# Three attentions: all turns of a pair in one place, the third and fourth group in the main banks, outputs turned back one pair later

## What is computed

```python
# window: 8 query heads, keys within 128 positions and 256 context keys, a sink column per head
s = where(|i - j| <= 128, q @ k.T * 64**-0.5, NEG);  p = softmax([s, s_ctx, sink])[..., :-1];  y = p @ v
# grid: 8 heads, keys in a neighbourhood of rows and columns, with a bias, and 256 context keys
s = q @ k.T * 64**-0.5 + bias;  p = softmax([s, s_ctx]);  y = p @ v
# dilated: 8 heads, a mixture of three dilations, written as one softmax over all earlier keys with log-multiplicities added
s = q @ k.T + log(multiplicity);  p = softmax(s);  y = p @ v
```

## Time and profile before

| | |
|---|---|
| Median of 3 runs | 2650.97 us (2650.01 to 2652.58) |
| Profiled execution | 2643.95 us, its span 2642.0 us |
| Granted TensorE clock, mean | 0.996 of 2.4 GHz |
| PE busy | 2573.2 us, 97% of the span |
| PEld busy | 1870.0 us, 71% |
| DVE, ACT, POOL busy | 58%, 30%, 8% |
| Chain that ended last | PE 92%, DVE 3%, issue 2%, ACT 2% |

### The profile page before, as it was taken

One profiled execution on the slowest core, in us unless ns is written; L12 is line 12 of the kernel. 1 busy time (PEld: TensorE's weight loads), 2 busy tenths in 40 slices (PEclk: granted clock), 3 DMA queues, 4 the chain that ended last, 5 costly groups with the idle time before them and its releaser, 6 DMA issues.

```text
span 2642.0 us, 37526 instructions
## 1 busy us (share of the span) xinstructions
PE 2573.2 (97%) x14026; PEld 1870.0 (71%) x14026; DVE 1539.8 (58%) x3920; ACT 804.4 (30%) x1740; POOL 223.7 (8%) x401
## 2 busy tenths in 40 slices
PE   6999999999999999999999999999999999999999
PEld 3577688777778685466688776868578766555867
DVE  2357677599866663434353476657868664515554
ACT  3236511176721123322210066113312264121210
POOL 1100000000011000000051031200000002002000
PEclk9999999999999999999999999999999999999999
DMA  7121000022013230211001110523240103316231
GB/s 275 36 79 48 21 33 32 32 73 73 18 52 108 66 106 28 100 41 41 9 25 38 50 34 30 92 80 107 85 144 32 68 18 98 119 53 250 95 113 56
DMA packets 73059, 188.78 MB, mean 71 GB/s; under 512 B 6988, under 2 KB 9744, under 8 KB 71952
## 3 DMA queue, kind: packets, MB, share of 16 engines
q0 software_dynamic: 26656, 94.84, 11.2%
q1 hardware_dynamic: 45472, 91.16, 9.9%
q10 hardware_dynamic: 752, 0.38, 0.1%
HBM read 143.69 MB, written 43.01 MB: 71 GB/s over the span
## 4 chain that ended last, share of the span: by engine, by line
PE 92%; DVE 3%; issue 2%; ACT 2%; DMA 0%; ACTq 0%; POOL 0%; DVEq 0%
PE psum L1378 36%; PE psum L1710 11%; PE psum L1650 8%; PE psum L1722 7%; PE psum L1740 5%; PE psum L1806 4%; PE psum L1737 4%; PE psum L1592 3%; PE psum L1492 3%; PE psum L1364 2%; PE psum L1345 1%; PE psum L1878 1%; PE psum L1896 1%; PE psum L1865 1%; PE psum L1625 1%
## 5 line engine op out<-in xcount | busy, mean ns | idle before, releaser
L3167 ACT ACTIVATE RP<-RP,small 128x1280 f32<-128x1280 f32 (+11 forms) x274 | 252.0, 920 | 165.4 <-DVE small L2725 161.5
L1710 PE MATMUL psum<-RQ 64*128 64x256 f32 (+5 forms) x1344 | 294.0, 498 | 2.0 <-DVE small L2725 1.2
L2725 DVE CUSTOM_DVE_ANT_0 RP<-psum,small 128x512 f32<-128x512 f32 (+1 forms) x382 | 201.8, 573 | 109.0 <-PE psum L1722 86.5
L1650 PE MATMUL psum<-RW,hT 128*128 128x512 f32 (+2 forms) x640 | 237.8, 527 | 1.0 <-ACT hT L2917 1.0
L1722 PE MATMUL psum<-ident,RP 128*128 128x128 f32 x1388 | 206.2, 283 | 9.1 <-DVE RP L2738 4.5
L1722 PEld LDWEIGHTS psum<-ident,RP 128*128 128x128 f32 x1388 | 151.3, 142 | 82.1 <-issue 68.5
L3179 ACT ACTIVATE RP<-psum 128x512 f32<-128x512 f32 (+1 forms) x288 | 150.1, 521 | 192.3 <-PE psum L1722 182.0
L1710 PEld LDWEIGHTS psum<-RQ 64*128 64x128 f32 (+1 forms) x1344 | 140.5, 189 | 88.2 <-issue 48.2
L1650 PEld LDWEIGHTS psum<-RW,hT 128*128 128x128 f32 x640 | 135.2, 215 | 87.5 <-issue 69.8
L1378 PE MATMUL psum<-RW,hT 128*128 128x256 f32 x864 | 195.9, 379 | 0.0
L1378 PEld LDWEIGHTS psum<-RW,hT 128*128 128x128 f32 x864 | 163.8, 190 | 25.0 <-issue 2.2
(11 more groups left out here) (485 smaller groups left out, 3937.1 us busy)
## 6 DMA issues: line engine op xcount, KB each, us to landing
RW<-in_w_in SPq DMA_DIRECT2D x7, 2048.0 KB, 8.0
RW<-in_od_w_ada SPq DMA_DIRECT2D x6, 2048.0 KB, 7.9
RW<-in_ev_w_in SPq DMA_DIRECT2D x5, 2048.0 KB, 7.7
RW<-in_od_w_in SPq DMA_DIRECT2D x5, 2048.0 KB, 7.9
RQ<-in_ev_w_ada SPq DMA_DIRECT2D x4, 2048.0 KB, 19.7
RX<-in_x POOLq DMA_DIRECT2D x12, 512.0 KB, 7.3
y_even<-YR POOLq DMA_DIRECT2D x20, 256.0 KB, 2.3
RP<-y_even POOLq DMA_DIRECT2D x20, 256.0 KB, 3.5
```

The source lines that it names most:

```text
L1650: last = pe.matmul(main.bank(f)[:, 0:nc_], lhs_of(st["lhs"], j["t"], kk), w, start=kk == 0, stop=kk == kn - 1)
L1710: last = pe.matmul(main.bank(f)[:, 0:pc["w"]], q, kk[:, keys], start=i == 0, stop=i == len(u["qk"]) - 1)
L2725: drained(main, dve.tensor_tensor_reduce(pair_slot(st, u, lane)[:, pc["at"]:pc["at"] + pc["w"]], main.bank(f)[:, 0:pc["w"]], add, -scale, ...
L3167: fn(pr, pr, ACT.Exp, bias=mins[:, at, lane, n - 1:n], scale=-1.0, accum_out=sums[:, at, lane:lane + 1]).then_inc(s_pexp, 1)
```

## The change

In the three attentions all chunks of a pair are turned in one place, behind the values of the pair before. The first two are fills of `turn` as before, the third and fourth are fills of `main`, numbered after the scores of the next pair. The first and third chunk are copied by ACT, the second and fourth by DVE. The turn-back of pair i - 2 (not i - 1) stands at the end of the round, and the last two pairs' turn-backs stand behind the loop. Each chunk now carries its ring (`ch["ring"]`), and all waits on chunks go through it. The latent attention keeps its loop, from which the branches of the other three are taken out; diff keeps its own.

The plan:

```diff
                 for c in range(n):
-                    side = "act" if c % 2 or (n == 3 and c == 2) or kind == "diff" else "dve"
-                    u["turns"].append({"f": turn.new(side), "c": chunk_count[0], "tiles": tiles[cuts[c]:cuts[c + 1]]})
+                    ch = {"ring": turn, "c": chunk_count[0], "tiles": tiles[cuts[c]:cuts[c + 1]]}
+                    if kind in HALVES and c >= 2:
+                        ch["ring"] = main
+                    elif kind in HALVES:
+                        ch["f"] = turn.new("dve" if c else "act")
+                    else:
+                        ch["f"] = turn.new("act" if c % 2 or (n == 3 and c == 2) or kind == "diff" else "dve")
+                    u["turns"].append(ch)
...
-                if at and kind in HALVES:
-                    pairs[at - 1]["back"] = main.new("dve")
+                if kind in HALVES:
+                    for c, ch in enumerate(u["turns"][2:]):
+                        ch["f"] = main.new("dve" if c else "act")
+                    if at >= 2:
+                        pairs[at - 2]["back"] = main.new("dve")
             if kind in HALVES:
-                pairs[-1]["back"] = main.new("dve")
+                for u in pairs[-2:]:
+                    u["back"] = main.new("dve")
```

PE:

```diff
+                    if k in HALVES:
+                        for i, u in enumerate(ps):
+                            for nxt in ps[i + 1:i + 2]:
+                                scores(nxt, nxt["pieces"])
+                            if i:
+                                pair_values(ps[i - 1], slice(None))
+                            for nxt in ps[i + 1:i + 2]:
+                                if nxt["aside"]:
+                                    modulation(*nxt["aside"])
+                            for ch in u["turns"]:
+                                turn_chunk(u, ch)
+                            if i >= 2:
+                                turn_back(ps[i - 2])
+                        turn_back(ps[-2])
+                        pair_values(ps[-1], slice(None))
+                        turn_back(ps[-1])
+                        continue
```

DVE and ACT:

```diff
+                    if k in HALVES:
+                        for i, u in enumerate(ps):
+                            for nxt in ps[i + 1:i + 2]:
+                                for c in range(len(nxt["pieces"])):
+                                    for lane in range(2):
+                                        minima(nxt, lane, c)
+                                if nxt["aside"]:
+                                    modulation(*nxt["aside"])
+                            divide(u)
+                            turned_chunks(u, u["turns"])
+                            if i >= 2:
+                                pair_y(ps[i - 2])
+                        for u in ps[-2:]:
+                            pair_y(u)
+                        continue
...
+                    if k in HALVES:
+                        for i, u in enumerate(ps):
+                            for nxt in ps[i + 1:i + 2]:
+                                exponential(nxt, 0)
+                            if i:
+                                pair_outputs(ps[i - 1])
+                            turned_chunks(u, u["turns"])
+                            for nxt in ps[i + 1:i + 2]:
+                                exponential(nxt, 1)
+                        pair_outputs(ps[-1])
+                        continue
```

More of the change, by code:

```diff
@@ L527, in plan_pairs @@
                 for c in range(n):
-                    side = "act" if c % 2 or (n == 3 and c == 2) or kind == "diff" else "dve"
-                    u["turns"].append({"f": turn.new(side), "c": chunk_count[0], "tiles": tiles[cuts[c]:cuts[c + 1]]})
+                    ch = {"ring": turn, "c": chunk_count[0], "tiles": tiles[cuts[c]:cuts[c + 1]]}
[6 more added lines that the diff above has]
+                    u["turns"].append(ch)
                     chunk_count[0] += 1
-                u["turned"] = [[ch["f"] for ch in u["turns"] if any(x[0] == lane for x in ch["tiles"])][-1:] for lane in range(2)]
+                u["turned"] = [[ch for ch in u["turns"] if any(x[0] == lane for x in ch["tiles"])][-1:] for lane in range(2)]
             def number_scores(u):
@@ L1192, in sink_columns @@
                         if u["at"] >= 3:
-                            turn.wait_full(gp, ps[u["at"] - 3]["turns"][-1]["f"])
+                            ch = ps[u["at"] - 3]["turns"][-1]
+                            ch["ring"].wait_full(gp, ch["f"])
                         else:
@@ L1719, in turn_chunk @@
                             pe.wait_ge(s_pexp, 2 * u["g"] + 1 + max(x[0] for x in ch["tiles"]))
-                        turn.wait_free(pe, ch["f"])
+                        ring = ch["ring"]
+                        ring.wait_free(pe, ch["f"])
                         for i, (lane, at, _) in enumerate(ch["tiles"]):
-                            last = pe.transpose(turn.bank(ch["f"])[:, i * P:(i + 1) * P],
+                            last = pe.transpose(ring.bank(ch["f"])[:, i * P:(i + 1) * P],
                                                 pair_slot(st, u, lane)[:, at:at + P], ident[:, :])
-                        turn.written(last)
+                        ring.written(last)
                     def pair_values(u, chunks):
@@ L1730, in pair_values @@
                         for ch in u["turns"][chunks]:
-                            turn.wait_drained(pe, ch["f"])
+                            ch["ring"].wait_drained(pe, ch["f"])
                             for i, (lane, at, kt) in enumerate(ch["tiles"]):
@@ L1786, in _ @@
                             turn_chunk(u, ch)
-                        if before and k in HALVES:
-                            turn_back(before)
                     for ch in ps[-1]["turns"][2:4]:
                         turn_chunk(ps[-1], ch)
[L1791 to L1796, removed]
+                    pair_values(ps[-1], slice(0, 1))
+                    turn_chunk(ps[-1], ps[-1]["turns"][4])
+                    pair_values(ps[-1], slice(1, None))
                 elif k == "ssm":
@@ L2711, in minima @@
                                 dve.wait_ge(s_mix, u["at"] - 2)
-                            for ft in ps[u["at"] - slots]["turned"][lane]:
-                                turn.wait_full(dve, ft)
+                            for ch in ps[u["at"] - slots]["turned"][lane]:
+                                ch["ring"].wait_full(dve, ch["f"])
                         add = pc["add"][lane] if k == "grid" and pc["add"] is not None else pc["add"]
@@ L2731, in turned_chunks @@
                         for ch in chunks:
-                            if turn.side[ch["f"]] != "dve":
+                            ring = ch["ring"]
+                            if ring.side[ch["f"]] != "dve":
                                 continue
-                            turn.wait_full(dve, ch["f"])
+                            ring.wait_full(dve, ch["f"])
                             if ch["c"] >= 4:
@@ L2737, in turned_chunks @@
                             n = len(ch["tiles"]) * P
-                            drained(turn, dve.tensor_copy(pair_turned(ch["c"])[:, 0:n], turn.bank(ch["f"])[:, 0:n]), ch["f"])
+                            drained(ring, dve.tensor_copy(pair_turned(ch["c"])[:, 0:n], ring.bank(ch["f"])[:, 0:n]), ch["f"])
                     def divide(u):
@@ L2810, in _ @@
                             minima(nxt, 0, 0)
[L2811 to L2812 removed]
                         if before:
                             turned_chunks(before, before["turns"][2:4])
[L2815 removed]
+                        if nxt:
                             minima(nxt, 1, 0)
[L2817 removed]
                             for c in range(1, len(nxt["pieces"])):
@@ L2823, in _ @@
                         if nxt and nxt["aside"]:
-                            if k == "latent" and before:
+                            if before:
                                 pair_y(before)
@@ L2828, in _ @@
                         turned_chunks(u, u["turns"][:2])
-                        if before and not (k == "latent" and nxt and nxt["aside"]):
+                        if before and not (nxt and nxt["aside"]):
                             pair_y(before)
@@ L3172, in turned_chunks @@
                         for ch in chunks:
-                            if turn.side[ch["f"]] != "act":
+                            ring = ch["ring"]
+                            if ring.side[ch["f"]] != "act":
                                 continue
-                            turn.wait_full(act, ch["f"])
+                            ring.wait_full(act, ch["f"])
                             if ch["c"] >= 4:
@@ L3178, in turned_chunks @@
                             n = len(ch["tiles"]) * P
-                            turn.consumed(fn(pair_turned(ch["c"])[:, 0:n], turn.bank(ch["f"])[:, 0:n], ACT.Copy), ch["f"])
```

(1 more changed line is left out.)

## The result

| | before | after |
|---|---|---|
| Median (5 runs each) | 2650.01 us (2649.21 to 2652.58) | 2663.9 us (2661.68 to 2666.24) |
| Ratio after / before | | 1.005, 95% interval 1.0035 to 1.0064 |
| Span of the profiled execution | 2642.0 us | 2661.8 us |
| PE busy | 2573.2 us | 2579.5 us |

The account below looks back on a forecast made before the run. TensorE (PE), busy 97% of the span, was taken as the bound. Turn-back 16.9, third and fourth chunk 5.6 and tails 1.5 sum to 24.0 us off the 2650.97 median: 2627.0 us, range 2623 to 2631.

Parts of the forecast that it names:

- Moved at no cost: Three attentions: chunk copies changing engine, later final multiplication and POOL's later block store cost nothing.
- Turn-back one pair later: All 104 pairs: turn-backs no longer wait for ACT's copy; 18.5 us gained, 16.9 net of short pairs.
- short pairs: Twelve pairs of 256 key columns, window and dilated: period 2.05 us, keeping 0.13 us each, 1.6 us in all.
- Third and fourth chunk: 64 pairs: turning these chunks with the others gains 9.6 us, less 4.0 of stalls, 5.6 net.
- tails: Last pair of each attention: third chunk's turn no longer finds both turn banks full; 1.5 us gained.
- The shape change: 64 pairs: one extra change of matmul shape saved, 0.15 us each, 9.6 us gross.
- the ring: Five main banks: the next scores wait for the third chunk's bank, 0.12 us per window pair, 4.0 us in all.
- Rival A: Main banks in 64 pairs: ACT frees the third bank later, eating the saving; 2633 to 2635 us, chance 0.26.
- Rival C: Third chunk's main bank: ACT copies it after the second exponential, scores stall 0.7 us per pair; 2666 us, chance 0.05.
- The clock: Half-clock stretch at the dilated attention's start: may end sooner or begin elsewhere, some 3 us either way; nothing taken.

Follow-up runs that it names:

- Experiment 1: The changed kernel with POOL's sink columns of the window attention issued one pair earlier: 2625.01 us, ratio 0.9905.
- experiment 2: The kernel before, with POOL's block store in the window attention also waiting until pair u + 2's first chunk is copied: 2689.06 us, ratio 1.0146.
- experiment 6: The kernel before with turn-back and final multiplication one pair later, chunks and POOL's sink columns as before: 2654.24 us, ratio 1.0026.
- experiment 4: The kernel before with turn-back and final multiplication one pair later and POOL's sink columns one pair earlier, chunks as before: 2632.39 us, ratio 0.9938.
- experiment 3: The changed kernel with turn-back, its numbering and final multiplication back at pair i - 1: 2641.91 us, ratio 0.9967.

## Why the prediction was wrong

**The step that failed** is "Moved at no cost", and in it the sentence that "POOL's store of a block come[s] one pair (2 to 6 us) later" with its cover: that a block's buffer is wanted only four pairs on and that POOL works only 14 us of the stretch. Both are true and beside the point. The store's wait stands in POOL's program ahead of the sink columns of pair u + 3, which ACT's exponential needs in the same round in which the turn-back of u is now made. I looked at who needs the data of the store and at how busy POOL is, and not at what is queued behind its wait; and the sink columns themselves I checked only for their own wait (the third chunk's turn, indeed earlier). In its place the runs show 36.1 us in which ACT waited for POOL's sink columns, nine stalls of PE, and 38.9 us of loss where the sentence had none. Experiment 1 takes out this one thing and gives 2625.0, experiment 2 puts it alone into the kernel before and gives the loss, experiment 6 shows that the later turn-back is what it hangs on.

The Trainium skill, TensorE: Matmul & The Clock Gate, "Architectural detail: the array is 16× 32×32, not 1× 128×128", has GpSimd's queues as strictly first in, first out. The trace agrees: at all nine places two or three sink columns start together just behind the store (218.71 behind 218.07).

**Turn-back one pair later, 18.5 us less 1.6 for short pairs.** Borne out as far as the scatter lets one see: 16.9 forecast, 17.0 by the medians of experiment 4, 15.0 by the lengths of its three attentions. Its gain doesn't lie in the long grid pairs, which stay at 4.02 us there, but in pairs with fewer key tiles (3.93 to 3.43 us in the grid attention). Short pairs: 2.05 forecast, 2.02 measured.

**Third and fourth chunk, 9.6 less 4.0, and tails 1.5.** 7.1 forecast; 7.5 in experiment 3 and 7.4 between experiments 4 and 1 by the medians, 6.3 and 8.0 by the lengths of the attentions. The shape change was sized rightly (a long grid pair 3.87 for 4.02), the ring too dear: it costs a long window pair 0.02 us and not 0.12, 2.4 us less over 24 pairs, because ACT's short instructions overlap where the prediction added them up. Against that, the two parts taken alone save less than the sum of their terms. The 24.4 us of experiment 1 beside the 24.0 forecast is therefore a sound mechanism with some luck in the sum.

**Rival A** named the right sign, scores that wait for ACT's chunk copy, with the wrong cause. In the changed kernel ACT's copies are late behind a late exponential; with POOL on time the same ring costs next to nothing (experiment 1). **Rival C**, the slower one, also had the main bank as its mechanism; it is ruled out as the cause by experiments 1 and 3, which have the bank and no such stall, though experiment 6 shows that the chunk part deepens the loss. None of the rivals had POOL in it.

**The clock** I had bounded at 3 us either way. It was some 17 of the 38.8 us lost in the window attention. I had also written that PE was without work ahead of the half clock of the earlier trace rows; the trace has it busy for 2.62 of the 4.10 us before.

**What stays open.** The division into 21.4 us of idle time and 17.4 us of slower matmuls is read from one profile of each kernel. How the clock's share goes with the length of the stalls was not set up as an experiment. Three profiles say something of it: with six stalls of about 1.6 us and three of 1.6 to 2.2 (experiment 6) the window attention was at half clock for 14.9 us, with nine of 2.4 to 2.6 (the changed kernel) for 32.1, and with nine of 2.9 to 3.0 (experiment 2) for 33.3, hardly more.

## What to carry to other kernels

When a wait is moved later, list for each engine that makes that wait the instructions behind it in its own program, and who needs them; an engine that is busy 9% of the time (POOL, 14.0 of 157.8 us) can still hold up the kernel, because what stands behind a wait in its program waits too. Look at the releaser's releaser: the row that shows PE's idle time named ACT's copy and the ring, and the cause stood two waits further back, at a store. And try the cure before giving up the idea: two lines in POOL's order turned 13.9 us of loss into 24.4 of gain.

## What was not expected of the hardware

A stall of about 2.5 us of PE, repeated every four pairs, cost most of its own length again in clock. In the changed kernel's window attention the granted clock was 0.50 (1.2 GHz) in seven stretches. Each begins at one of the nine stalls, from 0.5 us before its end to 1.7 us behind it; two stalls have none. One of the stretches, and the same time in experiment 1, where PE had not stopped:

```profile
242.90:249.70 6.80, 6.68 (x35) 5.21 (x37) 1.37 (x5) 3.33 (x9) 0.22 (x1) 0.50 0.00 0
```

```profile
242.90:249.70 6.80, 6.80 (x72) 5.10 (x71) 5.45 (x20) 4.33 (x13) 1.22 (x4) 1.00 0.11 40
```

In 6.8 us PE made 35 matmuls for 72, busy nearly all the time in both. The same groups of a long pair show the price, first in the changed kernel, then in experiment 1:

```profile
244.17 2.40 PE L1749 MATMUL psum<-RP,RQ 128*64 128x128 f32 x20
246.50 2.40 PE L1734 MATMUL psum<-ident,RP 128*128 128x128 f32 x10
```

```profile
244.39 1.31 PE L1749 MATMUL psum<-RP,RQ 128*64 128x128 f32 x20
245.63 1.31 PE L1734 MATMUL psum<-ident,RP 128*128 128x128 f32 x10
```

The values take 2.33 us from start to start at half clock and 1.24 at full clock. The Trainium skill, TensorE: Matmul & The Clock Gate, "Why this matters for your kernels", warns of idle gaps between bursts of matmuls in the middle of a kernel because they bring the clock down. The runs here agree in kind, though that section has longer gaps in mind than these of 2.4 to 2.6 us, and put the price at some 17 us beside 21.4 of idle time.
